# Two transformer blocks in one kernel: idle matmuls, last products by halves, and three reorderings of steps and weight splits

## The reference

```python
for l in range(2):                                    # first_block
    x = x + 0.5 * swiglu(rms_norm(x, ffn1_norm[l]), ffn1_w_gate_up[l], ffn1_w_down[l])
    u_ssd, u_ml, u_rw = split(rms_norm(x, mix_norm[l]) @ w_in[l])
    y = concatenate([ssd_mixer(u_ssd), mlstm_mixer(u_ml), rwkv7_mixer(u_rw)])
    x = x + y @ w_out[l]
    x = x + 0.5 * swiglu(rms_norm(x, ffn2_norm[l]), ffn2_w_gate_up[l], ffn2_w_down[l])
x = rms_norm(x, final_norm)
for l in range(2):                                    # second_block; m = silu(c) @ ada_w[l] + ada_b[l]
    x = x + 0.5 * m[2] * swiglu_2(rmsnorm(x) * (1 + m[1]) + m[0], ...)          # and ctx
    x = x + m[5] * (fourier_layer if l == 0 else retention_layer)(...)          # ctx in layer 0
    x = x + 0.5 * m[8] * swiglu_2(...)                                          # ctx in layer 0
return rmsnorm(x, final_g)
```

## Time and profile before

| | |
|---|---|
| median of 3 runs | 3462.03 us (3461.65 to 3463.73) |
| the profiled execution | 3463.73 us, its span 3461.7 us |
| PE busy | 3247.6 us, 94% |
| DVE busy | 2101.1 us, 61% |
| ACT busy | 1308.7 us, 38% |
| mean granted clock of PE | 0.972 |
| the chain that ended last | 64% PE, 25% DVE, 7% ACT |

### The profile page before, as it was taken

The page is one execution under the profiler, slowest core; times in us unless marked ns, Lnnn a source line. Parts: engine busy times, 40 slices in busy tenths (PEclk is TensorE's granted clock), DMA queues, the critical chain, the costliest instruction groups (busy, mean ns, idle before and its releaser), DMA issues.

```text
span 3461.7 us, 45970 instructions
## 1 busy us (share of the span) xinstructions
PE 3247.6 (94%) x19010; PEld 2824.2 (82%) x19010; DVE 2101.1 (61%) x2545; ACT 1308.7 (38%) x1584; POOL 115.8 (3%) x126
## 2 busy tenths in 40 slices
PE   7998988999998898899999999999999999999998
PEld 7978877898988786798788877788878888787797
DVE  6757557776866657677775754775343333544654
ACT  4434244444435234543421233422233122444443
POOL 0001200000000210000000000000000000000000
PEclk9999999999999998999999999999999999999999
DMA  6542022555553112455443531343222222323452
GB/s 250 230 152 86 27 95 77 200 235 204 211 207 104 38 60 72 177 208 211 153 164 123 183 124 37 122 165 122 91 85 98 91 98 80 118 98 109 164 183 98
DMA packets 83835, 462.96 MB, mean 134 GB/s; under 512 B 7573, under 2 KB 11285, under 8 KB 43562
## 3 DMA queue, kind: packets, MB, share of 16 engines
q1 hardware_dynamic: 77952, 451.45, 35.6%
q10 hardware_dynamic: 5674, 8.57, 0.8%
HBM read 458.95 MB, written 1.05 MB: 133 GB/s over the span
## 4 chain that ended last, share of the span: by engine, by line
PE 64%; DVE 25%; ACT 7%; issue 2%; DMA 0%; ACTq 0%; POOL 0%; DVEq 0%; POOLq 0%
PE ps L100 64%; DVE lo L311 8%; DVE acc L459 5%; ACT hi L305 3%; PE ps L546 1%; DVE acc L456 0%; DVE m0restMs L1980 0%; DVEq L86 0%; DVE xt L701 0%; DVE f11rot L875 0%; DVE f10rot L875 0%; DVE f20rot L875 0%; ACT f20hf_h L853 0%; ACT f11hf_h L853 0%; ACT f10hf_h L853 0%
## 5 line engine op out<-in xcount | busy, mean ns | idle before, releaser
L311 DVE TENSOR_TENSOR lo<-raw,hi 128x2048 fp32r<-128x2048 f32 (+1 forms) x357 | 809.6, 2268 | 622.8 <-ACT hi L305 601.5
L305 ACT ACTIVATE hi<-raw 128x2048 fp32r<-128x2048 f32 (+1 forms) x357 | 676.1, 1894 | 572.7 <-PE ps L100 541.9
L459 DVE SCALAR_TENSOR_TENSOR acc<-raw,sil,acc 128x512 f32<-128x512 f32 x504 | 379.0, 752 | 20.7 <-DVE f21hf_l L877 0.5
L100 PE MATMUL ps<-half00hs,hi 128*128 128x512 f32 x672 | 209.3, 393 | 0.6 <-DVE lo L311 0.6
L100 PE MATMUL ps<-half02hs,hi 128*128 128x512 f32 x672 | 209.0, 392 | 0.7 <-DVE lo L311 0.7
L100 PE MATMUL ps<-half10hs,hi 128*128 128x512 f32 x672 | 208.7, 392 | 0.8 <-DVE lo L311 0.7
L100 PEld LDWEIGHTS ps<-half10hs,hi 128*128 128x128 f32 x672 | 125.7, 188 | 28.5 <-DVE lo L311 1.6
L100 PEld LDWEIGHTS ps<-half02hs,hi 128*128 128x128 f32 x672 | 125.4, 188 | 27.6 <-DVE lo L311 1.1
L100 PEld LDWEIGHTS ps<-half00hs,hi 128*128 128x128 f32 x672 | 125.2, 188 | 27.3 <-DVE lo L311 1.0
L100 PE MATMUL ps<-half10hs,lo 128*128 128x512 f32 x352 | 137.6, 391 | 0.0
L100 PE MATMUL ps<-half02hs,lo 128*128 128x512 f32 x352 | 137.6, 391 | 0.0
(11 more groups left out here) (919 smaller groups left out, 7900.3 us busy)
## 6 DMA issues: line engine op xcount, KB each, us to landing
raw<-in_ffn_w_gate_up SPq DMA_DIRECT2D x88, 1024.0 KB, 9.0
raw<-in_ffn_gu SPq DMA_DIRECT2D x88, 1024.0 KB, 5.0
raw<-in_ffn_w_down SPq DMA_DIRECT2D x85, 1024.0 KB, 5.2
raw<-in_ada_w SPq DMA_DIRECT2D x72, 1024.0 KB, 5.1
raw<-in_w_in_t SPq DMA_DIRECT2D x28, 1024.0 KB, 5.0
raw<-in_ret_w_in SPq DMA_DIRECT2D x24, 1024.0 KB, 4.9
raw<-in_w_out SPq DMA_DIRECT2D x16, 1024.0 KB, 5.0
raw<-in_w_in_n SPq DMA_DIRECT2D x12, 1024.0 KB, 5.0
```

The source lines that it names most:

```text
L100: return p().matmul(o, l, r, start=start, stop=stop, skip_group_check=True)
L305: a().activation(self.high(w), self.raw[self.place(r)][:, 0:width], ACT.Copy).then_inc(*a.mark(self.wac, w))
L311: v().tensor_tensor(self.low(w), self.raw[self.place(r)][:, 0:width], self.high(w).bitcast(F32), ALU.subtract).then_inc(*v.mark(self.wdv, w))
L459: v().scalar_tensor_tensor(out=acc[:, n, :], in0=w[:, k, :], scalar=s, in1=acc[:, n, :], op0=ALU.mult, op1=ALU.add).then_inc(*v.mark(self. ...
```

## The change

It has these parts:

- **Idle matmuls.** `Core.idle(p, bank, n)` issues n fp32 matmuls of 128x256 on constants, with no wait of their own. They stand ahead of the wait for `xs` in eleven of the twelve norms (8 or 9 in those of 256 rows of the first network, 23, 13 or 15 in the second), in `ProjRw` (8), `Prep` (4), `Rest` (4), `Inv` (11 for each of two halves), `Scan` before `Yc`'s transposes (11), `Ssd` (13 and 8), and `Out` (twice 6). That is 78 for a mixer with its norm, and 276 in all.
- **Last products by halves.** In `Ffn`, `MixOut`, `Out` and `Fourier`, the last group of tiles goes through the banks one by one (row tile, half of the width, tiles) rather than (row tile, tiles, halves). The bank of a row tile's first half is then complete 12 matmuls before the second half's, not 3.
- **Prep.** Four `tensor_scalar` on DVE (line 1219) become four `Identity` with scale and bias on ACT; DVE computes the bias in one instruction on 4 columns.
- **Splits.** `Rest.hold` goes from one entry to four, and the copy to `KBV` is ahead of a weight's `lo` and of the convolutions.
- **The mixer's order.** The last 16 steps of `Rest` (letter p below) and `conv` stand among the first steps of `Ssd`; `Ssd` (s) is finished before most of `Mlstm` (m), and the pieces of `MixOut` (o) are spread over both.
- **f21.** `soon` is gone: `Ada` phases follow two of three gate tiles rather than three of four. After the down products of 256 rows, `Ada` phases follow every second group rather than every third.
- **Fourier, retention.** `Fourier`'s phases have another order against `Gates`; the last two phases of `Ret` alternate with the first of `Out`.

```diff
+    def idle(self, p, bank, n):
+
+        for _ in range(n):
+            mm(p, self.ps[bank][:, 0:256], self.ones, self.msk[:, 0:2, :].rearrange("p a b -> p (a b)"))
...
         K.ada.clear(p)
+        if self.idle:
+            if len(self.rows) == 4 and not self.turn[0]:
+                self.before[0].row(p, 0, 1)
+            K.idle(p, *self.idle)
         p.wait_ge(*self.dv["xs", self.turn[-1]])
...
                 if ends:
-                    order = [(a, t) for t in range(nt) for a in parts]
+                    order = [(a, t, [h]) for t in range(nt) for h in range(2) for a in parts]
...
+            if q == 2:
+                self.K.idle(p, 2, 8)
             project_t(self, p, self.M.hx, self.norm, q, q, self.K.ps[q % 4])
...
-        for c in range(4):
-            v().tensor_scalar(M.ch[:, c, :], M.ab[:, c, :], 1.0, K.col(l, "ka", c), ALU.subtract,
-                              ALU.mult).then_inc(*v.mark(D, "ka", c))
...
             x.then_inc(*p.mark(E, "bv", T))
+            K.idle(p, 1, 11)
             p.wait_ge(*D["bv", T])
...
+        K.idle(p, 0, 11)
         p.wait_ge(*D["Yn", 1])
...
-    his, phases, places, hold = 2, 112, 3, {1: 4}
+    his, phases, places, hold = 2, 112, 3, {1: 4, 5: 33, 6: 42, 8: 59}
...
+            if n == 0:
+                p.wait_ge(*A["xt", 3])
+                K.idle(p, 0, 13)
...
+        p.wait_ge(*D["across", 0])
+        K.idle(p, 1, 8)
         p.wait_ge(*D["yn", 3])
...
+                if j == 0:
+                    K.idle(p, 2, 6)
                 p.wait_ge(*self.dv["ys", j // 4])
...
-                elif j % (4 if soon else 3) < (3 if soon else 2):
+                elif j % 3 < 2:
                     fill()
...
-                    if s.nt == 2 and g[0] % 3 == 0:
+                    if s.nt == 2 and g[0] % 2 == 0:
                         fill()
...
-        for i in range(10):
-            run(rest)
-        beside(scan, 10)
-        conv(2)
-        for s in "osmsmsmsmsmsmsmsmsmsmsmsmsmsmsmsmomomomomoo":
-            run({"s": ssd, "m": ml, "o": out}[s])
+        run(scan)
+        conv()
+        for s in "pppppppp" "sppppsppppc" "sssmsmosmsmsmsmsmsmsmsmsmsmm" "omommomommomo":
+            run({"s": ssd, "m": ml, "o": out, "p": rest, "c": ev}[s])
```

More of the change, by code:

```diff
@@ L817, in tensor @@
                     rows = slice(t * 128, (t + 1) * 128)
-                    for h in range(2):
+                    for h in hs2:
                         c = slice(h * 512, (h + 1) * 512)
@@ L1110, in tensor @@
         yield
+        K.idle(p, 7, 4)
         p.wait_ge(*A["sq"])
@@ L1175, in scalar @@
         a().activation(t2[0:8, 0, :], ps[0][0:8, 0:256], ACT.Sqrt).then_inc(*a.mark(self.ac, "norm"))
+        a.wait_ge(*self.dv["nka"])
+        for c in range(4):
+            a().activation(M.ch[:, c, :], M.ab[:, c, :], ACT.Identity, scale=K.col(l, "ka", c),
+                           bias=self.nka[:, c:c + 1]).then_inc(*a.mark(self.ac, "ka", c))
         yield
@@ L2314, in tensor @@
         yield
-        p.wait_ge(*self.ssd.dv["lo", 7])
         for q in range(7):
             parts = [(q + i, c) for i in range(2 if q == 6 else 1) for c in range(2)]
-            order = [(a, t) for t in range(2) for a in parts] if q == 6 else [(a, t) for a in parts for t in range(2)]
-            for at, ((n, c), t) in enumerate(order):
+            order = ([(a, t, [h]) for t in range(2) for h in range(2) for a in parts] if q == 6 else
+                     [(a, t, range(2)) for a in parts for t in range(2)])
+            for at, ((n, c), t, hs) in enumerate(order):
                 wh, wl = (w.rearrange("p (c n) -> p c n", n=1024)[:, c, :] for w in self.ready(p, n))
@@ L2322, in tensor @@
                 first, last, rows = (n, c) == (0, 0), (n, c) == (7, 1), slice(t * 128, (t + 1) * 128)
-                for h in range(2):
+                for h in hs:
                     s = slice(h * 512, (h + 1) * 512)
+                    if first:
+                        p.wait_ge(*self.ssd.dv["lo", 4 * t + 2 * h + 1])
                     x = mm3(p, K.ps[2 * t + h][:, :], yh[:, rows], yl[:, rows], wh[:, s], wl[:, s], first, last)
@@ L2329, in tensor @@
                         x.then_inc(*p.mark(self.pe, "back", t, h))
-                if q == 6 and t == 0 and last:
+                if q == 6 and t == 0 and h == 1 and last:
                     yield
@@ L2568, in scalar @@
                     if g == 4:
-                        if s == 0:
-                            a.wait_ge(*self.second.all)
-                            a().activation(self.wxs[0][0:5, :], self.wx[0:5, :], ACT.Copy).then_inc(*a.mark(A, "wx"))
                         a.wait_ge(*self.dv["e", n])
@@ L2575, in scalar @@
                     self.squares(a, 1)
+                elif (s, i) == (0, 15):
+                    a.wait_ge(*self.second.all)
+                    a().activation(self.wxs[0][0:5, :], self.wx[0:5, :], ACT.Copy).then_inc(*a.mark(A, "wx"))
                 if i in (7, 15, 20):
@@ L2964, in first @@
         s.since = since
+        norm.idle = None if before is setup else (0, 9) if which == 1 else (4, 9)
         if before is setup:
@@ L2978, in mixers @@
                                   K.at(ROWS + 8192, f"mn{l}no", 3, 512), lambda c, s: K.col(l, "nm", c)))
+        norm.idle = 0, 8
         prw = put(f"prw{l}", ProjRw(K, l, M, norm))
@@ L3015, in mixers @@
         conv()
-        beside(inv, 1, 1)
+        beside(inv, 1, 1, 1)
         conv()
-        beside(inv, 1, 2)
+        beside(inv, 2)
         conv()
@@ L3079, in network @@
                                  (ROWS, 50176), 16384, [2, 3, 0, 1])
-    ffn(s, [norm, norm], soon=True, late=8)
+    norm.idle = 0, 23
+    ffn(s, [norm, norm], late=8)
     fill_to(18)
@@ L3087, in network @@
     four = put("four", Fourier(K, "four", half, 0, both, Gated(gates, both, rot)))
-    for s in (half, half, four, half, half, four, four, gates, four, four, gates, four, gates, four, gates, four, gates):
+    for s in (half, half, four, half, half, four, gates, four, gates, four, four, four, gates, four, gates, four, gates):
         run(s)
@@ L3094, in network @@
                                  90112)
+    norm.idle = 0, 13
     join(four, norm)
@@ L3100, in network @@
                                  (45056, 67584), 69632)
+    norm.idle = 0, 15
     join(before, norm)
@@ L3113, in network @@
     gates = put("retgates", Gates(K, "retg", [ret], 1, 1, 1, 1.0, gb, dg, 3))
-    rout = put("retout", Out(K, "retout", [ret], A["ret_w_out_2"][0], yT, ys, Gated(gates, K.xa, rot), 6))
+    rout = put("retout", Out(K, "retout", ret, A["ret_w_out_2"][0], yT, ys, Gated(gates, K.xa, rot), 6))
+    norm.idle = 0, 15
     join(half, norm)
-    for _ in range(ret.phases):
+    for _ in range(ret.phases - 2):
         run(ret)
-    for q in range(rout.phases - rout.tail):
+    for s in (rout, ret, rout, ret, rout, gates, rout, gates, rout, gates):
+        run(s)
+    for _ in range(rout.phases - rout.tail - 5):
         run(rout)
-        if q < 3:
-            run(gates)
     norm, gates, half = half_ffn(1, 2, 2, [22], K.xa, rout, 8192, 16384, (53248, 61440), 69632, 79872, 75776, (8192, 30720),
```

120 lines of the change are left out of this document (69 added, 51 removed).

## The result

The changed kernel takes 3502.72 us (median of 4 runs, 3500.45 to 3504.48) against 3461.84 us: ratio 1.0116, 95% interval 1.0102 to 1.013. It is 41 us slower, where I had forecast 81 us less.

The account below looks back on a forecast made before the run. PE's own work, 3247.6 us, was the floor, with 214 us idle and 194 at half clock to win from. Mixers 49.3, joins 12.9, norms 3, f21 12, Fourier 2, retention 5, overruns -3: 81.2 us off, 3381 us, range 3350 to 3420.

Parts of the forecast that it names:

- the price: Norms and mixers: 276 idle matmuls at 0.215 us each take 59.3 us of PE time, free if ending before the wait.
- Rival (a): The clock isn't held: idle products end 1.5 to 1.7 us before the wait does; 3400 us, chance 0.09.
- the 0.985 that I had asked for: Sign over the whole kernel that the forecast holds: a mean clock of 0.985 or more.
- Rival (b): Transposes let the clock fall, so idle products hold it only where products follow; 3388 us, chance 0.03.
- KBV: Mixers' inverse: the copy could come some 3.8 us sooner; with the clock 5.8 us a mixer, bounds 2 and 7.5.
- ssd, mlstm and the output product: Mixer's end: the new order mixes w_out's products with ssd's dense DVE work; 14 us a mixer, bounds 7 and 20.
- rival (c): The reorderings of the mixer's end give nothing; 28 us are missing, 3409 us, chance 0.15.
- (d): Mixer's end: 13 weight splits a mixer fall uncovered in ssd's dense part, costing 60 us; 3469 us, chance 0.04.
- Joins by halves: Twelve joins: DVE's first-half work leaves the path, 0.75 us each for six, 1.4 for six gated; sum 12.9 us.
- Prep: Mixers' prep: DVE loses four instructions of 1.53 us; 1.5 us a mixer, bounds 0 and 1.9.
- f21: MLP f21: its acc waits of 8.0 us, absent in f20, go; 12 us, bounds 9 and 13.3.
- Fourier and retention: PE's wait for fx_l no longer ahead of all output products, 2 us; gaps and half clock at retention's end, 5.

Follow-up runs that it names:

- the old list: Changed kernel with the mixer's list of phases and Rest.hold of before: 3465.42 us with all idle matmuls, 3441.83 with half, 3450.32 with none.
- the old hold: Changed kernel with Rest.hold of before alone: 3487.69 us, ratio 1.0072.
- the string alone: Changed kernel with the mixer's list of before from the recurrence on, but ssd, mlstm and output product in the new order: 3501.38 us.

## Why the prediction was wrong

Forecast and measurement are 122 us apart. The terms outside the idle matmuls and the mixer's list were to give 34.9 us (joins 12.9, f21 12, Fourier and retention 7, prep 3), and the kernel with those alone gained 11: 23 of the 122. Idle matmuls and list were to give the other 46.3 and cost 52: the remaining 99.

**The step that failed first** is the price: "Eight fp32 products of 256 columns start 1.72 us before the next eight, 0.215 each; 276 are 59.3 us". The rows count records; the program has four products where they say x8. Each is 0.43 us, all are 119, where the sum had 59.3. Of the claim "They cost nothing as long as they end before the wait does", the condition then fails nearly everywhere: 8 take 3.4 us in a gap of 3.20, 11 take 4.8 in 4.03, 15 take 6.5 us ahead of `half10`, whose wait was 4.8. The overruns were put at 3 us; the idle matmuls cost 15 us net in the old list, after all that they give back, and 37 in the new one. That they hold the clock was right, where they ran: in the projection there is no half clock left. Rival (a), that they don't, fell by the clock, 0.987 in the old list with them and 0.975 without. The 0.982 of the changed kernel is under the 0.985 that I had asked for. Rival (b), transposes that let the clock fall, fell too: 16 transposes behind idle products ran in 1.91 us at a granted clock of 1.00, and the projections behind them did as well.

The Trainium skill's sentence on this (TensorE: Matmul & The Clock Gate, Part 4, that the full clock does not engage for transposes in PE's transpose mode) is not borne out by these 1.91 us, nor by the clock that rose in the midst of transposes alone; the traces don't say whether the kernel's transposes are of that mode.

**KBV.** "What is late next is the split, which then waits for nobody on PE within the inverse" was true word for word and useless: DVE waits for the split, and PE for what stands behind it on DVE. The waits of 7.5 us went, and 8.9 us of waits for `yT` and the state came. Forecast was a gain of 5.8 us a mixer; the stretch from there to the recurrence grew from 78.5 to 87.8 us, 9.3. It takes both the idle matmuls and the late split: 79.3 us without the first, 79.4 with the old hold.

**ssd, mlstm and the output product.** Forecast 14 us a mixer. From the recurrence's start to the next norm's transposes mixer 0 takes 188.8 us, where it took 177.3. The alternation costs 10 to 11 us a mixer; for this term rival (c), that the new order gives nothing, was the nearest, and still too kind. I had argued from DVE's slack that mixing in the output product would cover ssd's waits, "since the order changes at each of the places where PE waits"; the order also changed which step stands between two steps of the same chain, and the waits for `Ms`, `ml` and `vw` grew from 0.6, 2.3 and 0.5 to 4.9, 4.5 and 2.8 us with the string alone. That this is because ssd and mlstm alternate less is argued; the runs show only that the string does it. My case for the slower side, (d), had the right stretch and, in its 3469 us, the time nearest to the measured one, but a wrong mechanism: from `Yc`'s transposes to the next norm's, PE waits for `lo` for 2.7 us in the changed kernel and 2.2 before (37.4 and 36.9 over the whole span).

**Joins by halves.** "The first can now run while PE does the second half's 12 matmuls, so half, 0.75 us, leaves the path": it was off the path already. DVE's pair started at 224.78, before PE's last products had ended, because the first half was complete three matmuls earlier. For the MLPs' ten joins, some 11 of the 12.9 us, the kernel's time shows nothing; the other two joins were not run alone.

**Prep.** 0, not 1.5 a mixer: the lower bound that I gave, by the stall that I named.

**f21.** In its own stretch the mechanism was right, and the size nearly: 8.6 us of 12, and 2.0 were given back in f20. Over the kernel the edit alone shows 3 us, not told from none.

**Fourier and retention.** The wait for `fx_l` is gone. Their single effects were not measured by themselves. Without idle matmuls and with the old list, all the rest of the change is worth 11 us. There f21's stretch is 9.3 us shorter, Fourier's 3.4 (503.1 for 506.5) and retention's 3.1 (309.9 for 313.0); but Fourier's takes 506.5 without idle matmuls in the new list too, with the same code, so how the 11 us divide is open.

**The range** was too narrow because each bound came from the kernel of before with one edit at a time. Neither the doubled price nor two edits that remove one wait was in any of the cases.

## What to carry to other kernels

Before a filler is priced from a trace, count its records against the program's instructions; a row's "x8" may be four instructions. Fill a wait once: where one edit removes a wait and another fills it, price them together, since the filler then stands on the path. When an instruction is moved out of the way on an engine in order, ask when its own input is ready at the new place and read everything behind it; and keep two dependent chains alternating step by step unless a run has shown otherwise.

## What the runs showed of the hardware

An fp32 matmul of 256 columns is recorded as two of 0.215 us, 0.43 in all, where one of the split fp32r products of as many columns takes 0.12. Idle matmuls hold the clock, and about as well at half the number: 0.986 against 0.987 over the kernel, and 0.975 with none. They hold it for transposes that come right behind (1.91 us for 16, where it was 2.66). And waiting can have a second price of about its own size: in the one stretch where it was measured, the mixer's end, 4.8 us more of waits came with 5.1 us more of busy time for the same instructions, at a clock of 0.94 and not 0.99.
